# Adding the expert outputs to their tokens' rows: by products and vector additions, or by indirect accumulating DMAs into memory

## What is computed

```
logits = t @ w_router                      # 256 tokens, 8 experts
top_vals, top_idx = top_k(logits, 2)       # two experts a token
gates = sum(one_hot(top_idx) * softmax(top_vals))
for e in range(8):                         # width of an expert: 3584
    out = out + gates[:, e:e+1] * ((silu(t @ w1[e]) * (t @ w3[e])) @ w2[e])
x = layer_norm(alpha * x + out)            # then the per-layer input gate
```

## Time and profile before

| | us |
|---|---|
| median of 3 runs | 2615.81 (2614.94 to 2616.8) |
| the profiled execution, its own time | 2615.35 |
| its span in the profile | 2613.7 |
| stretch of the experts' units, about | 1604 to 2567 |
| PE busy over the span | 2589.9 (99%) |
| DVE busy | 2030.6 (78%) |
| ACT busy | 1609.4 (62%) |
| POOL busy | 237.6 (9%) |

### The profile page before, as it was taken

How to read it: one execution, slowest core, us unless ns; L and a number is a source line. 1 busy time by engine, 2 the same in 40 slices (tenths; PEclk the granted TensorE clock), 3 DMA queues, 4 the chain that set the end, 5 groups by cost and what they waited for, 6 DMA issues and landing times.

```text
span 2613.7 us, 42275 instructions
## 1 busy us (share of the span) xinstructions
PE 2589.9 (99%) x17032; PEld 2235.0 (86%) x17032; DVE 2030.6 (78%) x2920; ACT 1609.4 (62%) x2362; POOL 237.6 (9%) x236
## 2 busy tenths in 40 slices
PE   9999999999999999999999999999999999999999
PEld 8999899999877779999888887888888888888887
DVE  7667676776755547678766788999999999999997
ACT  6557655555542235553555536887788778787875
POOL 1102000000111217001610100000000000000000
PEclk9999999999999999999999999999999999999999
DMA  7554255455421135563455545999999999999994
GB/s 287 191 182 141 97 197 190 173 185 192 141 83 65 52 130 185 186 220 105 161 192 193 179 150 204 373 369 349 357 370 367 351 353 372 363 367 360 363 367 166
DMA packets 85383, 609.58 MB, mean 233 GB/s; under 512 B 9608, under 2 KB 9864, under 8 KB 12224
## 3 DMA queue, kind: packets, MB, share of 16 engines
q1 hardware_dynamic: 82656, 596.35, 62.1%
q10 hardware_dynamic: 2176, 7.32, 0.8%
q0 software_dynamic: 352, 3.15, 0.3%
HBM read 605.73 MB, written 1.05 MB: 232 GB/s over the span
## 4 chain that ended last, share of the span: by engine, by line
PE 94%; DVE 4%; ACT 1%; issue 1%; DVEq 0%; ACTq 0%
PE bank L441 93%; PE bank L3274 1%; DVE weights_lo L431 0%; ACT weights_hi L423 0%; DVE mean L582 0%; PE bank L2147 0%; DVE rstd L498 0%; DVE weights_hi_scratch L2331 0%; DVE weights_hi_scratch L2291 0%; ACT squares L480 0%; DVE arena L591 0%; DVE x_T L914 0%; DVE arena L2633 0%; DVE source L665 0%; PE bank L1194 0%
## 5 line engine op out<-in xcount | busy, mean ns | idle before, releaser
L431 DVE TENSOR_TENSOR weights_lo<-raw_weights,weights_hi 128x1024 fp32r<-128x1024 f32 x816 | 1002.5, 1248 | 355.4 <-ACT weights_hi L423 350.1
L423 ACT CAST weights_hi<-raw_weights 128x1024 fp32r<-128x1024 f32 x816 | 847.9, 1050 | 299.3 <-PE bank L441 282.5
L441 PE MATMUL bank<-source,weights_hi 128*128 128x512 f32 (+1 forms) x2464 | 571.9, 362 | 3.2 <-DVE source L968 2.3
L441 PEld LDWEIGHTS bank<-source,weights_hi 128*128 128x128 f32 x2464 | 427.0, 190 | 65.2 <-issue 4.1
L441 PE MATMUL bank<-weights_hi,source 128*128 128x512 f32 (+1 forms) x1280 | 387.5, 386 | 2.3 <-DVE source L665 1.0
L431 DVE TENSOR_TENSOR weights_lo<-arena,weights_hi 128x1024 fp32r<-128x1024 f32 x278 | 335.9, 1224 | 30.5 <-ACT weights_hi L423 27.0
L441 PE MATMUL bank<-source,weights_lo 128*128 128x256 f32 x2112 | 345.0, 282 | 0.0
L423 ACT CAST weights_hi<-arena 128x1024 fp32r<-128x1024 f32 x278 | 292.3, 1054 | 50.4 <-PE bank L441 35.9
L441 PEld LDWEIGHTS bank<-source,weights_lo 128*128 128x128 f32 x2112 | 307.5, 191 | 17.3 <-DVE weights_lo L431 0.2
L441 PEld LDWEIGHTS bank<-weights_hi,source 128*128 128x128 f32 x1280 | 231.4, 188 | 46.7 <-issue 3.1
L441 PE MATMUL bank<-weights_lo,source 128*128 128x512 f32 (+1 forms) x640 | 243.4, 380 | 0.0
(11 more groups left out here) (353 smaller groups left out, 3395.5 us busy)
## 6 DMA issues: line engine op xcount, KB each, us to landing
raw_weights<-in_exp_in SPq DMA_DIRECT2D x134, 1024.0 KB, 6.4
arena<-in_exp_in SPq DMA_DIRECT2D x90, 1024.0 KB, 6.3
raw_weights<-in_exp_w SPq DMA_DIRECT2D x67, 1024.0 KB, 6.2
arena<-in_exp_w SPq DMA_DIRECT2D x45, 1024.0 KB, 6.4
raw_weights<-in_ffn_w_down SPq DMA_DIRECT2D x44, 1024.0 KB, 5.0
raw_weights<-in_ffn_w_up SPq DMA_DIRECT2D x43, 1024.0 KB, 4.9
raw_weights<-in_ffn_w_gate SPq DMA_DIRECT2D x42, 1024.0 KB, 4.8
raw_weights<-in_dense_w SPq DMA_DIRECT2D x33, 1024.0 KB, 4.8
```

What stands on the lines that cost most here:

```text
L423: k.act.copy(k.weights(j)[0], raw_half(k, j)).then_inc(k.w_hi_ready, 1)
L431: k.dve.tensor_tensor(lo, raw_half(k, j), hi.bitcast(F32), ALU.subtract).then_inc(k.w_ready, 1)
L441: return k.pe.matmul(dst, lhsT, rhs, start=start, stop=stop, skip_group_check=shared)
```

## The change

For experts 0 to 6 the products of `scatter` on PE, the low part of y and the additions on VectorE go away. z of 256 rows, and 128 spare rows behind them, now lies in a tensor in HBM, `moe_sums`. GpSimd stores alpha times x there (one DMA of 1 MiB). When an expert is through, ScalarE writes gate times y as plain 32-bit floats (`y_rows`, the same two instructions, no rounding), and GpSimd issues one indirect DMA: 128 rows of 4 KB each, each added to the row of its token in `moe_sums`. It waits for each before it issues the next. In unit 8 of expert 7 ScalarE waits for the seventh, and issues a DMA of 1 MiB that brings the sums back into z. `last_scatter` is as before, but waits for that landing.

The row numbers (`row_of_slot`) come from the gather: the small product that gave the slot's gate has three columns instead of one (gate, token number, 1), and ScalarE makes from them, with two more instructions an expert, the token's row, or the spare row of the slot where it is empty. A table (`slot_table`, 128x50) is loaded for it, and VectorE has two more small copies in the routing.

```diff
+        self.z_rows = nc.dram_tensor("moe_sums", (T + P, D), F32, kind="Internal").ap()
...
+    k.dve.wait_ge(k.moe_landed, 48)
+    k.dve.tensor_copy(k.row_of_slot[:, :], t.spare_row.to_broadcast([P, E])).then_inc(*k.route_dve.step("spare rows"))
...
-    chained(k.dve.tensor_tensor(t.gates, t.first, t.second, ALU.add), "gates")
+    chained(k.dve.tensor_tensor(t.gates, t.first, t.second, ALU.add), "gates of experts")
+    chained(k.dve.tensor_copy(t.of_token[:, :, 0], t.gates), "gates")
...
@@ own_gather_tensor
-        k.pe.wait_ge(*ve.at(("y", 2 * p - 2, 1)))
+        k.pe.wait_ge(*k.rows_out.at(2 * p - 2))
-            ins = mm(k, bank[:, T:T + 1], pick[:, tt * T + at:tt * T + at + P], t.gates[:, tt * E + e:tt * E + e + 1],
+            ins = mm(k, bank[:, T:T + 3], pick[:, tt * T + at:tt * T + at + P], t.of_token[:, tt * E + e, :],
...
@@ own_gather_scalar
         k.act.copy(t.own_gate[e % 4], bank[:, T:T + 1])
+        if e < ADDED_BY_DMA:
+            k.act.activation(t.rest_of_row[e], bank[:, T + 2:T + 3], ACT.Identity, bias=t.spare_row, scale=t.minus_spare)\
+                .then_inc(*sc.step(("spare_row", e)))
+            k.act.wait_ge(*sc.at(("spare_row", e)))
+            k.act.activation(k.row_of_slot[:, e:e + 1], bank[:, T + 1:T + 2], ACT.Identity, bias=t.rest_of_row[e], scale=1.0)
...
@@ own_tensor
-        if e - 1 in SCATTER_AFTER and 3 <= i < 7:
-            scatter(SCATTER_AFTER[e - 1], i - 3)
...
@@ own_scalar, down(n), last unit of an expert
+            if e >= 2:
+                k.act.wait_ge(k.rows_added, 16 * (e - 1))
+            for c in range(2):
+                ins = k.act.activation(t.y_rows[e % 2][:, c * 512:(c + 1) * 512], k.bank[2 * (e % 2) + c][:, :], ACT.Copy,
+                                       scale=t.own_gate[e % 4])
+            ins.then_inc(*k.rows_out.step(e))
...
+        if e == E - 1 and i == SUMS_AT:
+            k.act.wait_ge(k.rows_added, 16 * ADDED_BY_DMA)
+            k.act.dma_start(tokens_of(t.z), rows_of(k.z_rows)).then_inc(k.sums_landed, 16)
...
@@ own_vector
-        if i in (1, 2) and e > 0:
-            y_low(e - 1, i - 1)
-        if e - 1 in SCATTER_AFTER and 3 <= i < 7:
-            spare = scatter(SCATTER_AFTER[e - 1], i - 3, spare)
...
@@ gpsimd_program
+    k.pool.dma_start(rows_of(k.z_rows), tokens_of(moe_z(k))).then_inc(k.sums_stored, 16)
+    k.pool.wait_ge(k.sums_stored, 16)
+    for e in range(ADDED_BY_DMA):
+        k.pool.wait_ge(*k.rows_out.at(e))
+        k.pool.indirect_dma_start(k.z_rows, bass.IndirectOffsetOnAxis(ap=k.row_of_slot[:, e:e + 1], axis=0),
+                                  MoeTiles(k).y_rows[e % 2], None, bounds_check=T + P - 1, oob_is_err=True,
+                                  compute_op=ALU.add).then_inc(k.rows_added, 16)
+        k.pool.wait_ge(k.rows_added, 16 * (e + 1))
```

More of the change, by code:

```diff
@@ L132, in constant_arrays, with slot_table @@
                                          axis=1),
-            "inverse_count": np.ascontiguousarray(count), "expert_rows": pick.reshape(N_EXPERTS, -1)}
+            "inverse_count": np.ascontiguousarray(count), "expert_rows": pick.reshape(N_EXPERTS, -1),
+            "slot_table": slot_table()}
+def slot_table():
+    token = np.arange(T).reshape(TT, P).T
+    of_token = np.zeros((P, TT, N_EXPERTS, 3), np.float32)
+    of_token[:, :, :, 1] = token[:, :, None]
+    of_token[:, :, :, 2] = 1.0
+    spare = (T + np.arange(P, dtype=np.float32))[:, None]
+    return np.concatenate([of_token.reshape(P, -1), spare, -spare], axis=1)
 def bucket_of_distance():
@@ L327, in __init__ @@
         self.moe_base, self.moe_summed = track("moe_base_ready"), sem("moe_sums_done")
+        self.rows_out, self.rows_added = track("expert_rows_ready"), sem("expert_rows_added")
+        self.sums_stored, self.sums_landed = sem("moe_sums_stored"), sem("moe_sums_landed")
         stream = stream_order()
@@ L2380 @@
 TE_TAPS = 13
+SLOT_TABLE = 3 * 2 * N_EXPERTS + 2
 VP, UP = T + PAD_CONV, T + PAD_POOL
@@ L2857, in __init__, with tokens_of, rows_of @@
         self.own_gate = [table[:, 49 + i:50 + i] for i in range(4)]
+        self.rest_of_row = [table[:, 106 + e:107 + e] for e in range(E)]
+        self.of_token = table[:, 56:56 + 3 * 2 * E].rearrange("p (n i) -> p n i", i=3)
+        self.spare_row, self.minus_spare = table[:, 104:105], table[:, 105:106]
+        self.y_rows = [k.arena[:, 5 * KT * T + i * D:5 * KT * T + (i + 1) * D] for i in range(2)]
         self.z = moe_z(k)
+def tokens_of(z):
+    return z.rearrange("p (t d) -> p t d", t=TT)
+def rows_of(z):
+    return z[0:T, :].rearrange("(t p) d -> p t d", p=P)
 def by_tile(z):
@@ L2873, in moe_tables_load @@
     k.act.dma_start(t.rows, k.dram["expert_rows"]).then_inc(k.moe_landed, 16)
+    at = 4224 + 56
+    k.act.dma_start(k.arena[:, at:at + SLOT_TABLE], k.dram["slot_table"]).then_inc(k.moe_landed, 16)
 def repeated(z):
@@ L3094, in all_scalar @@
             split_both(split_hi, k, EXPERT_DOWN, i - 1)
+    for _ in range(ADDED_BY_DMA):
+        k.act.copy(t.rest_of_row[0], t.spare_row).then_inc(k.rows_out.semaphore, 1)
     last_splits(k, split_hi, 2)
@@ L3140 @@
 PICK_AT = GATHER_AT - 2
-SCATTERED = ((0, 1), (2, 3), (4, 5), (6,), (7,))
-SCATTER_AFTER = {group[-1]: g for g, group in enumerate(SCATTERED)}
+SUMS_AT = 8
+ADDED_BY_DMA = E - 1
+SPARE_ROWS = P
 START_BANKS = 6
@@ L3226, in own_pick_vector @@
     if p == 0:
-        k.dve.wait_ge(k.moe_landed, 32)
+        k.dve.wait_ge(k.moe_landed, 48)
         k.dve.wait_ge(*k.route_dve.at("places"))
@@ L3303, in last_scatter @@
     def last_scatter():
-        e, before = E - 1, SCATTER_AFTER[E - 1] - 1
+        e = E - 1
+        k.pe.wait_ge(k.sums_landed, 16)
         for c in range(2):
@@ L3307, in last_scatter @@
                 u = 2 * c + tt
-                k.pe.wait_ge(*ve.at(("z", before, u)))
                 if c:
@@ L3318, in last_scatter @@
                 ins.then_inc(k.moe_summed, 1)
[L3320 to L3330, removed]
     last = E * EXPERT_UNITS - 1
@@ L3372, in down @@
             last_splits(k, split_hi)
-        if i == EXPERT_UNITS - 1:
-            k.act.wait_ge(*(k.taken(EXPERT_DOWN, n) if n < last else mt.at("y0")))
+        if i == EXPERT_UNITS - 1 and e < ADDED_BY_DMA:
+            k.act.wait_ge(*k.taken(EXPERT_DOWN, n))
             k.act.wait_ge(*sc.at(("back", e)))
             if e >= 2:
-                k.act.wait_ge(*mt.at(("z", (e - 2) // 2 if e < E - 1 else 2, 3)))
+                k.act.wait_ge(k.rows_added, 16 * (e - 1))
[3 more added lines that the diff above has]
+            ins.then_inc(*k.rows_out.step(e))
+        elif i == EXPERT_UNITS - 1:
+            k.act.wait_ge(*mt.at("y0"))
+            k.act.wait_ge(*sc.at(("back", e)))
+            k.act.wait_ge(k.rows_added, 16 * (e - 1))
             for c in range(2):
@@ L3424, in y_low @@
             .then_inc(*ve.step(("y", e, c)))
[L3426 to L3433, removed]
     last = E * EXPERT_UNITS - 1
```

12 lines of the change are left out of this document (6 added, 6 removed).

## The result

| | before | changed |
|---|---|---|
| median, us | 2616.42 (2614.94 to 2621.1, 6 runs) | 2602.2 (2601.32 to 2608.05, 6 runs) |
| profiled execution, us | 2615.35 | 2602.16 |
| its span, us | 2613.7 | 2600.7 |

The ratio is 0.9945, 95% interval 0.9935 to 0.9954: the change takes off about 14 us, 0.55% (12 to 17 us by the interval). Between the profiled executions it is 13.19 us. The forecast was 2604.3.

What follows compares the result with a forecast made beforehand. The prediction took PE to bound the expert units, with the DMA engines close behind. From 2615.35 us, -12.76 + 0.3 + 0 + 1.0 = -11.5 gave 2603.9, and 0.46 for the median 2604.3; range 2601.5 to 2620.

Steps and rivals of the forecast that it cites:

- PE sets the pace, and the products are the gain: Expert units: PE bounds them, so removing 56 products, all on the path, saves 12.76 us.
- VectorE's 21.3 us worth nothing: Expert units: removing 16 additions and 14 low parts frees 21.3 us of VectorE but saves no time, since VectorE isn't late.
- ScalarE's additional instructions at the gathers: Gathers: two tiny instructions an expert, 0.45 us each expert, 0.9 a gather, absorbed at cost 0; 2.7 us at most.
- +0.3 us in the routing: Routing: VectorE's two small copies, 0.17 to 0.2 us each, put 0.3 us on the path (0 to 0.4).
- An accumulating DMA takes 2.8 to 4.4 us of engine time: After each of experts 0 to 6: it keeps weights away 2.8 to 4.4 us, swallowed and made good before the next.
- +1.0 us for it in experts 6 and 7: Experts 6 and 7, without gathers and with the load of the sums: the DMAs cost 1 us (0 to 6).
- 3% of room: DMA engines in the expert units: at most 386 GB/s with no gap, 3% above what PE asks for.
- The hold from which the change isn't worth anything: Experts: 6 us of each accumulating DMA's hold is absorbed; at 7.8 us the loss equals the 12.76 us gain.
- a hold of 11.1 us: Rival, each accumulating DMA blocks the engines for its whole landing: 36 us lost, about +23 net, 2638 us; chance 0.16.
- The first rival: Expert units: DMA engines become the bound by bytes alone, 957 us at 378 GB/s; 2606 to 2622, likeliest 2610; chance 0.21.
- No rounding waits for them: Sign of being right: weight loads land some us later after each expert's end, yet ScalarE's roundings never wait for them.

Runs made afterwards that it cites:

- e3: Changed kernel with VectorE's 14 low parts and 16 additions put back, results unused, without PE's products: median 2603.92 us, ratio to before 0.9951.
- e2: Changed kernel with the 56 products put back on PE in the same units, results unused: median 2615.42 us, ratio to before 1.0.
- e1: Changed kernel without its seven accumulating DMAs, outputs of experts 0 to 6 left out: median 2602.96 us, ratio to before 0.9951.

## Why the prediction was right, and where it was off

**PE sets the pace, and the products are the gain: shown.** The term was 12.76 us; 962.06 - 949.12 = 12.94. Of this 12.69 are the 16 units (9.34 and 8.89 to 8.43). Some 0.2 are the 0.02 to 0.04 us in one unit at each expert's beginning, a cost of VectorE's low parts that the prediction didn't have: with them back in e3 these units are 8.45 and 8.46 again, and in e2, without them, 8.43. The first unit (0.10 shorter) and the one of 8.49 (0.06 longer) nearly cancel. e2 against e1 brings the same 12.69 back in the same 16 units.

**VectorE's 21.3 us worth nothing: shown** by e3, but for these 0.2 us.

**ScalarE's additional instructions at the gathers: cost nothing, as put, but their size was wrong.** Between the start of the copy of one column and that of the picks lay 0.06 us before (1596.39 to 1596.45), and 0.61 and 0.62 lie there now (1597.46 to 1598.07, 1598.32 to 1598.94): 0.55 us an expert instead of the 0.45 estimated. All three gathers in the units still take 13.56.

**+0.3 us in the routing: the step held and its effect on the end didn't.** From VectorE's own_x_lo (1586.87 before, 1587.66 after) to its first low part of weights (1591.08, 1592.15) it is 0.28 us more; the 0.8 us by which the changed kernel is late at 1587.66 were there before VectorE's first new copy. But the first transposes of a unit start 0.11 us earlier than before. Between lies a stretch in which before ScalarE waited for PE in the middle of three roundings (1.34 us), and after it waits once and does three in a row. Why PE gave the places back sooner there isn't settled; no run was made for it.

**An accumulating DMA takes 2.8 to 4.4 us of engine time: measured 3.3.** The choice of the rows nearest in bytes rather than of GpSimd's landing times held. There was some luck in it, as the prediction had no row of such a DMA. The landing time (8.2 us; 14.3 for the first) is not what the weights lose.

**+1.0 us for it in experts 6 and 7: measured 0.** This is the term that was mis-sized, and with the 0.3 it is 1.3 of the 1.7 us by which the forecast was high: it expected 11.5 us off in the profiled execution, and 13.19 came. The rest is the 0.2 of the low parts and the 0.15 outside the span. The pauses of the gathers turned out not to be needed: experts 6 and 7, which have none, run at 8.43 throughout, with the adds of experts 5 and 6 and the load of the sums in them. e1 against the changed kernel: 0.04 us for all seven.

**The margin was under-estimated.** The prediction read the best stretch, 378 GB/s at a share of 0.98, as nearly the limit, and so gave the DMA engines 3% of room. But in that stretch nothing asked for more: SP was waiting for slots. With a backlog they made 404 to 418. The hold from which the change isn't worth anything was put at 7.8 us; the runs show a loss of 0.6 us an expert at 8.7 and of 2.5 at 11.2, break-even near 10.4. For a hold of 11.1 us the prediction counted 36 us of loss; at 11.2 it was 17.35. But these are several adds with pauses between them, so they don't measure the prediction's single hold; what they do show is that engine time isn't lost one to one. The first rival falls by the same rows: its 957 us of bytes took 378 GB/s for a ceiling, and the last 89 us ran at 390.

**What would show it.** The units, the missing rows and the chain came as written. The loads landed later behind each add, as it said. "No rounding waits for them" did not come: seven did. The sentence drew the line at the wrong engine; the waits that count are PE's.

## What to carry to other kernels

When PE sets the pace and the weights come through a ring of slots, work can be moved from PE to the DMA engines at a profit, as long as one such DMA takes less of the engines' time than the landed pieces lie ready (here 3.3 us against 3 to 5: where it was 3, the reserve was used up and 0.06 us came through once). Read that margin as lying time plus what the rate gains under a backlog, not as what is missing to a share of 1. Do not count on PE to regain what it has lost. And read the period on the engine that sets the pace, since the engines ahead of it show delays that never arrive.

## Of the hardware, not expected

- An indirect accumulating DMA of 128 rows of 4 KB takes 3.3 us of the 16 engines and lands in 8.2 us (14.3 the first); the same rows just written 1.35 and 4.5. GpSimd's instruction takes 1.54 against 0.97 us.
- The DMA share doesn't tell room: 0.99 at 375 GB/s, 0.99 at 386 and 1.01 at 417 in the same 30 us of three kernels.
- Delay put on the loads is lost late and not in proportion: one, two, three and four such DMAs in a row, 3.3, 6.1, 8.7 and 11.2 us of engine time an expert, cost 0.01, 0.2, 0.6 and 2.5 us.
